# Encoder layer on one core: the projection's begin in another order, softmax reciprocals stored as rows, the output norm in place

## The chip, the cores and the metric

The kernel runs on one NeuronCore of a Trainium2 chip. The metric is the device time of one execution in microseconds (us). In the text PE is TensorE, DVE is VectorE, ACT is ScalarE, POOL is GpSimd, and SP is the engine whose only work here is to issue DMAs; its queue and POOL's are the two queues of data transfers.

## The reference, cut to what matters

One encoder layer over 1024 "sample" and 512 "prompt" tokens of width 1024, in float32, after an input layer norm:

```python
x = LN(x; ln_in)                                      # input norm
u, q_lat, kv_lat, k_rope = split(x @ w_in)            # 512 + 384 + 256 + 32 columns
pool = pool_mixer(u)                                  # windows of 2, 4, 8, 16 tokens
attn = 8-head attention(rms(q_lat) @ w_uq, rms(kv_lat) @ w_ukv, rope)   # softmax
x = LN(alpha*x + [pool | attn] @ w_o; ln1)
aff = softmax(x @ w_router); each of 16 experts takes its top tokens
x = LN(alpha*x + sum over experts of gate * FFN(x); ln2)                # output norm
```

## The kernel before, in words

The program has four phases, one after the other, each with its own order of work written out by hand for each engine; engines meet only at semaphores, and between phases at a barrier. Tokens are worked on in 12 tiles of 128. Every float32 product is made of three passes (`three_passes`, L74 to L76): each operand is rounded to a "hi" part by ACT, and DVE subtracts to get the rest, the "lo" part; hi by hi, hi by lo and lo by hi are summed. So each operand costs an ACT copy and a DVE subtraction ahead of its matmuls.

**Projection** (`phase_project`). SP loads x in tiles, the norm's gain and bias (both spread to 128 partitions), and `w_in` in eight pieces of 128 rows (592 KB each) through a ring of five slots: piece c may only be loaded when DVE is done with piece c-5 (`load_w`). DVE takes a tile's statistics (L370, L373), POOL turns the variance into a reciprocal deviation (L248, L250), DVE normalises in two instructions (L381: subtract the mean and scale by the deviation; L384: multiply by the gain), and POOL adds the bias (L254). PE transposes the tile (L499), ACT rounds the transposed tile (L293), DVE takes its rest (L390). ACT rounds each piece of `w_in` (L299) and DVE takes its rest (L447); the transposed tiles 0 and 1 are rounded after pieces 3 and 6. Then PE makes, for each block of two tiles, the latents of each tile (`latents`, 48 matmuls: two halves of columns, eight pieces each, three passes) and the inputs of the pool mixer (`pool_inputs`, 48 matmuls a half), and transposes the latents (L538), for which DVE scales them (`scale_latents`, L397 to L412) with factors that POOL makes (`latent_rms`, L258, L260). The first product of latents waits for the pieces' rests one by one. The blocks are run in a hardware loop of two passes of two blocks, and a last pair written out.

**Attention** (`phase_attention`) goes over four pairs of heads, three in a hardware loop and one written out, in 20 steps a pair. The probabilities are not normalised: DVE stores the reciprocals of the row sums into `inv_sum`, a token per partition (`rest_probsT`, L940). After each of the six blocks of 512 queries SP stores the block's output (L745) and then its reciprocals, 128 partitions x 4 numbers, to `inv` in device memory (L751). There each number stands by itself: 24 such transfers of 512 numbers of 4 bytes.

**Mix** (`phase_mix`) loads the attention's output and the reciprocals, now as rows spread to 64 partitions (`load_mix`, L1266, L1269), multiplies them on DVE (L1418), and makes the product with `w_o` (loaded at L1277, rounded by ACT at L1378, rest by DVE at L1435). Norm, router and top-k follow.

**Experts** (`phase_experts`) ends with the output norm (`OutputNorm`). Its 12 tiles are read from `acc` in device memory (L1712) into six slots and written by DVE into six others: DVE takes statistics (L1794, L1797) and makes (a - mean) * gain (L1803), POOL the reciprocal deviation (L1729, L1731), then either ACT scales (L1779) and POOL adds the bias (L1738), or, for tiles 3, 8 and 11, DVE does both at once (L1812). For tiles 2, 5, 7 and 10 ACT makes the statistics (`sums`, L1760 to L1764). SP loads tile t+6 when tile t's product is made, and behind each such load stands the store of tile t (L1717) in SP's queue, which waits for that tile to be finished.

Of the kernel before, what the change touches and what calls it, by code (L numbers as in the profile page):

```python
# [87 lines left out]
def phase_project(nc, ident, dram, late, handed):  # L88

    with ExitStack() as ctx:  # L90
# [37 lines left out]
        consts_loaded, ln_loaded = m.sem("a_consts_loaded"), m.sem("a_ln_loaded")  # L128
        w_loaded = [m.sem(f"a_w_loaded{s}") for s in range(RING)]
# [19 lines left out]
        X0T_AFTER = (3, 6)  # L149
# [7 lines left out]
        def _(sp):  # L157
# [3 lines left out]
            for s in range(2):  # L161
                load_x(dram["x_sample"][s * P:(s + 1) * P, :], s)
# [11 lines left out]
            for dst, name in ((ln_g, "ln_in_g"), (ln_b, "ln_in_b")):  # L174
                sp.dma_start(dst[:, :], dram[name].partition_broadcast(P)).then_inc(ln_loaded, 16)
# [7 lines left out]
            for c in range(RING, KD + KVT_):  # L183
                load_w(c)
# [6 lines left out]
            def x_moves(j, s):  # L191

                if j + 1 < N_BLOCKS:
                    sp.wait_ge(x_centred, 2 * j + s + 1)
                    load_x(rows_of(2 * j + 2 + s), s)
# [44 lines left out]
        def _(pool):  # L240
# [11 lines left out]
            def add_bias(j, s):  # L252
                pool.wait_ge(x_scaled, 2 * j + s + 1)
                pool.tensor_tensor(x0[:, s, :], x0[:, s, :], ln_b[:, :], ALU.add).then_inc(x0_done, 1)  # L254
# [10 lines left out]
            pool.wait_ge(ln_loaded, 32)  # L265
            for s in range(2):
                add_bias(0, s)
            for s in range(2):
                reciprocal_std(1, s)
            add_bias(1, 0)  # L270
# [13 lines left out]
            with pool.Fori(0, PAIRS - 1) as i:  # L284
                step(i)
# [3 lines left out]
        def _(act):  # L289
# [6 lines left out]
            for c in range(KD + KVT_):  # L296
# [3 lines left out]
                else:  # L300
                    act.activation(wv_hi[:, c - KD, :], w_raw[:, c % RING, 0:512], ACT.Copy).then_inc(w_hi_done, 1)
                if c in X0T_AFTER:
# [34 lines left out]
            def step(i, last=False):  # L337
                for b in range(2):
# [3 lines left out]
                    for s in range(2):  # L342
# [3 lines left out]
                        round_x0T(j + 1, s, 1 - b)  # L346
                    for s in range(2):
                        copy_v(j, s, ps_u[s])

            with act.Fori(0, PAIRS - 1) as i:  # L350
# [12 lines left out]
        def _(dve):  # L363
# [74 lines left out]
            for s in range(2):  # L438
                statistics(0, s)
            dve.wait_ge(filled, 4)  # L440
            dve.wait_ge(ln_loaded, 32)
            for s in range(2):
                normalise(0, s)
            for c in range(KD + KVT_):
# [7 lines left out]
                if c in X0T_AFTER:  # L452
                    rest_x0T(0, X0T_AFTER.index(c), 0)
            dve.wait_ge(consts_loaded, 64)
            for s in range(2):
                statistics(1, s)
            normalise(1, 0)

            def step(i, positions, last=False):
                for b in range(2):  # L460
                    j = 2 * i + b
                    final = last and b == 1
                    scale_latents(j, 0, positions + 2 * b)
                    if not final:
# [6 lines left out]
                    rest_qT(j, 0)  # L471
                    if not final:
# [13 lines left out]
            with dve.Fori(0, PAIRS - 1) as i:  # L486
# [4 lines left out]
        def _(pe):  # L491
# [11 lines left out]
            def latents(j, s, slot):  # L503
# [5 lines left out]
                for h, (c0, c1) in enumerate(((POOL_DIM, POOL_DIM + SPLIT), (POOL_DIM + SPLIT, IN_DIM))):  # L509
                    for k in range(KD):  # L510
                        if isinstance(t, int) and t == 0 and h == 0:
                            pe.wait_ge(w_lo_done, k + 1)
# [66 lines left out]
            with pe.Fori(0, PAIRS - 1) as i:  # L579
# [13 lines left out]
def phase_attention(nc, ident, dram, late, handed):  # L593

    with ExitStack() as ctx:
# [36 lines left out]
        def half_place(n, h):  # L632
# [16 lines left out]
        row_sum, inv_sum = m.sb("row_sum", [P, 4]), late.inv_sum  # L649
# [36 lines left out]
            m.sem("b_" + x) for x in ("o_done", "inv_done", "o_low_copied", "o_added"))  # L686
        o_stored = [m.sem(f"b_o_stored{s}") for s in range(2)]
# [1577 lines left out]
```

## Time and profile before

| what | value |
| --- | --- |
| times of three runs | 1364.32, 1365.85, 1369.1 us; median 1365.85 us |
| the profiled execution | 1366.01 us, of which the span of its instructions is 1363.9 us |
| mean granted clock of PE | 0.95 |
| PE busy | 1195.7 us, 88% of the span |
| DVE, ACT, POOL busy | 67%, 50%, 27% of the span |
| projection, about | 2 to 232 us |
| attention, about | 233 to 596 us |
| mix, router and top-k, about | 597 to 848 us |
| experts, about | 848 to 1318 us |
| output norm, about | 1318 to 1364 us |

A busy share is a mean over stages with different limits; what a change is worth is read in its own stage, from who waits for whom. Times in the rows are us from the start of the span.

### The profile page before, as it was taken

What the parts mean: (1) busy time and instruction counts of PE and PEld (TensorE: products, weight loads), DVE (VectorE), ACT (ScalarE), POOL (GpSimd) and SP (SyncE); (2) the same over time, 40 slices, a digit from 0 to 9 for tenths busy, and PEclk for the clock granted to TensorE, in tenths of its full rate; (3) what the DMA queues carried; (4) which work ended last, traced back from release to release, by engine and by line L of the source; (5) the groups of instructions that cost most, each with busy time, mean ns of one, the idle gap of its engine ahead of it and who ended that gap; (6) DMA issues with size and microseconds to landing.
All of it is one profiled execution on the core that took longest, in us unless ns stands there. A gap on an engine that the chain in (4) does not pass through costs nothing. (4 is left out here: it accounts for less than half of the span.)

```text
span 1363.9 us, 22070 instructions
## 1 busy us (share of the span) xinstructions
PE 1195.7 (88%) x7370; PEld 1073.6 (79%) x7370; DVE 920.3 (67%) x1539; ACT 684.9 (50%) x1183; POOL 372.7 (27%) x437
## 2 busy tenths in 40 slices
PE   3899997799999999949999962999999999999950
PEld 2899987588788888837787741999999999999940
DVE  7555542477878778746545785777777777777746
ACT  4222221366666676633222222766666666766634
POOL 2222210233523000001221115333334333334217
PEclk9999998799999999979999975999999999999985
DMA  8244463955525111039545453898888998888747
GB/s 260 91 151 150 150 222 134 336 77 102 84 57 84 17 35 32 9 87 285 158 153 163 153 204 96 254 273 283 270 253 275 266 277 281 267 254 274 192 126 268
DMA packets 173743, 242.18 MB, mean 178 GB/s; under 512 B 25856, under 2 KB 135936, under 8 KB 173696
## 3 DMA queue, kind: packets, MB, share of 16 engines
q1 hardware_dynamic: 163840, 206.97, 48.2%
q0 software_dynamic: 9856, 34.61, 11.4%
q8 instruction: 26, 0.43, 0.2%
q14 instruction: 21, 0.17, 0.1%
HBM read 179.37 MB, written 62.18 MB: 177 GB/s over the span
## 5 line engine op out<-in xcount | busy, mean ns | idle before, releaser
L2125 PE MATMUL ps_gate_up<-xT_hi_lo,w_hi 128*128 128x384 f32 x896 | 261.3, 355 | 1.4 <-DVE xT_hi_lo L2050 1.4
L2126 PE MATMUL ps_gate_up<-xT_hi_lo,w_lo 128*128 128x192 f32 x896 | 224.5, 251 | 0.0
L2045 DVE TENSOR_TENSOR w_lo<-w_raw,w_hi 128x2048 fp32r<-128x2048 f32 x93 | 212.2, 2282 | 0.0
L1985 ACT ACTIVATE w_hi<-w_raw 128x2048 fp32r<-128x2048 f32 x92 | 175.7, 1910 | 0.0
L2126 PEld LDWEIGHTS ps_gate_up<-xT_hi_lo,w_lo 128*128 128x128 f32 x896 | 170.7, 191 | 0.6
L2125 PEld LDWEIGHTS ps_gate_up<-xT_hi_lo,w_hi 128*128 128x128 f32 x896 | 168.7, 188 | 2.3 <-issue 1.6
L931 DVE TENSOR_REDUCE neg_max<-ps_scores 128x1 f32<-128x1024 f32 (+1 forms) x80 | 97.6, 1220 | 41.6 <-PE ps_scores L76 41.1
L831 ACT ACTIVATE pT_hi<-ps_probsT 128x512 fp32r<-128x512 f32 x160 | 87.0, 596 | 71.6 <-PE ps_probsT L1058 71.2
L1901 POOL TENSOR_TENSOR d_wait_carrier<-d_zero 128x1 f32<-128x1 f32 x78 | 33.5, 429 | 289.1 <-PE ps_xT L2114 148.0
L944 DVE TENSOR_TENSOR pT_lo<-ps_probsT,pT_hi 128x512 fp32r<-128x512 f32 x160 | 101.3, 673 | 3.9 <-ACT pT_hi L831 3.9
L840 ACT ACTIVATE probs<-ps_scores,neg_max 128x1024 f32<-128x1024 f32 (+1 forms) x96 | 93.5, 979 | 14.6 <-DVE neg_max L931 14.3
L74 PE MATMUL ps_mix<-w_hi,mix_hi 128*128 128x512 f32 x192 | 79.6, 414 | 21.6 <-DVE w_lo L1435 18.6
L1058 PEld LDWEIGHTS ps_probsT<-ident,probs 128*128 128x128 f32 x640 | 72.7, 140 | 26.9 <-DVE pT_lo L944 14.6
L1058 PE MATMUL ps_probsT<-ident,probs 128*128 128x128 f32 x640 | 84.0, 274 | 10.7 <-ACT probs L840 9.9
L75 PE MATMUL ps_mix<-w_lo,mix_hi 128*128 128x512 f32 x192 | 76.2, 397 | 0.0
L76 PE MATMUL ps_mix<-w_hi,mix_lo 128*128 128x512 f32 x192 | 76.1, 396 | 0.0
L74 PE MATMUL ps_scores<-k_hi,q_hi 128*128 128x512 f32 x160 | 65.3, 408 | 1.6 <-DVE q_lo L925 1.6
L74 PE MATMUL ps_lat<-w_in_hi,x0T_hi 128*128 128x384 f32 (+1 forms) x192 | 63.0, 328 | 4.0 <-DVE k_rope_twice L412 3.4
L75 PE MATMUL ps_scores<-k_lo,q_hi 128*128 128x512 f32 x160 | 63.6, 397 | 0.0
L76 PE MATMUL ps_scores<-k_hi,q_lo 128*128 128x512 f32 x160 | 63.2, 395 | 0.0
L75 PE MATMUL ps_lat<-w_in_lo,x0T_hi 128*128 128x384 f32 (+1 forms) x192 | 61.8, 322 | 0.0
L76 PE MATMUL ps_lat<-w_in_hi,x0T_lo 128*128 128x384 f32 (+1 forms) x192 | 61.4, 320 | 0.0
(268 smaller groups left out, 3146.6 us busy)
## 6 DMA issues: line engine op xcount, KB each, us to landing
w_raw<-in_w_gate SPq DMA_DIRECT2D x32, 1024.0 KB, 8.1
w_raw<-in_w_up SPq DMA_DIRECT2D x32, 1024.0 KB, 8.5
w_raw<-in_w_down SPq DMA_DIRECT2D x32, 1024.0 KB, 7.0
scratch_x<-x SPq DMA_DIRECT2D x24, 512.0 KB, 2.7
scratch_v<-v_out SPq DMA_DIRECT2D x12, 512.0 KB, 4.8
v_hi_lo<-scratch_v SPq DMA_DIRECT2D x8, 768.0 KB, 13.0
x_again<-scratch_x SPq DMA_DIRECT2D x12, 512.0 KB, 3.7
scratch_acc<-acc_out SPq DMA_DIRECT2D x12, 512.0 KB, 3.1
```

The source lines that it names most:

```text
L74: nc.tensor.matmul(out, a_hi, b_hi, start=first, stop=False)
L75: nc.tensor.matmul(out, a_hi, b_lo, start=False, stop=False)
L76: return nc.tensor.matmul(out, a_lo, b_hi, start=False, stop=last)
L831: act.activation(pT_hi[unit % 2][half_place(n, h)], ps_t[h][:, :].rearrange("p (k t) -> p k t", t=P), ACT.Copy).then_inc(t_hi_done, 1)
L840: last = act.activation(probs[:, n % 2, x * width:(x + 1) * width], ps_s[n % 2][:, x * width:(x + 1) * width], ACT.Exp, bias=neg_max[:, n ...
L931: nc.vector.tensor_reduce(neg_max[:, n % 2, 0:count], ps_s[n % 2][:, :].rearrange("p (x c) -> p x c", x=count), op=ALU.max, axis=AX.X, neg ...
L944: nc.vector.tensor_tensor(pT_lo[unit % 2][at], ps_t[h][:, :].rearrange("p (k t) -> p k t", t=P), f32(pT_hi[unit % 2][at]), ALU.subtract).t ...
L1058: last = nc.tensor.transpose(ps_t[h][:, k * P:(k + 1) * P], probs[:, n % 2, (4 * h + k) * P:(4 * h + k + 1) * P], ident[:, :])
L1985: act.activation(w_hi[c][:, :], raw[:, c, :], ACT.Copy).then_inc(hi_done, 1)
L2045: nc.vector.tensor_tensor(w_lo[c][:, :], raw[:, c, :], f32(w_hi[c][:, :]), ALU.subtract).then_inc(lo_done, 1)
L2125: nc.tensor.matmul(ps[:, 0:2 * N], w_hi[chunk][:, at], xT[:, k, :], start=k == 0, stop=False)
L2126: nc.tensor.matmul(ps[:, 0:N], w_lo[chunk][:, at], xT[:, k, 0:N], start=False, stop=False)
```

## The change

It has four parts.

1. **The projection's begin.** SP's loads are in another order: tile 0 of x, gain, bias, tile 1, five pieces of `w_in`, then tiles 2 and 3 of x between the other pieces; the tables and gains of the latents and the two pieces for the values come behind. Tiles 0 and 1 are normalised on DVE alone, in two instructions of another kind: (x - mean) * gain, then times the deviation plus bias. The transposed tiles 0 and 1 are rounded after pieces 0 and 3. The first latents take both halves of columns for each piece. The pieces for the values are rounded inside the first block. POOL makes the first latents' factors ahead of the bias of tile 2.
2. **Projection without a hardware loop:** all blocks are written out.
3. **Reciprocals as rows.** `inv_sum` is kept for a whole pair of heads; PE transposes it at the pair's end, ACT copies the 24 x 128 result from PSUM, and SP stores it in one transfer of 24 rows of 512 bytes: 4 transfers instead of 24.
4. **The output norm in place.** Twelve slots, one for each tile, in which all its steps work; SP issues all loads, then all stores. ACT makes the statistics of tiles 2, 4, 6, 8 and 10, DVE ends tiles 3, 6, 9 and 11.

The instructions of DVE at the projection's begin, before (ps_transpose is the transposed tile, w_in_lo the pieces' rests, w_v_lo those of the pieces for the values):

```order
L381 TENSOR_SCALAR x<-x_in,ln_moments,ln_rstd 128x1024
L384 TENSOR_TENSOR x<-x,ln_in_g_all 128x1024
L447 TENSOR_TENSOR w_in_lo<-w_in_raw,w_in_hi 128x1184 x4
L390 TENSOR_TENSOR x0T_lo<-ps_transpose,x0T_hi 128x4x128 x2
L447 TENSOR_TENSOR w_in_lo<-w_in_raw,w_in_hi 128x1184 x3
L390 TENSOR_TENSOR x0T_lo<-ps_transpose,x0T_hi 128x4x128 x2
L447 TENSOR_TENSOR w_in_lo<-w_in_raw,w_in_hi 128x1184
L450 TENSOR_TENSOR w_v_lo<-w_in_raw,w_v_hi 128x512 x2
```

And in the changed program:

```order
L460 SCALAR_TENSOR_TENSOR x<-x_in,ln_moments,ln_in_g_all 128x1024
L466 SCALAR_TENSOR_TENSOR x<-x,ln_rstd,ln_in_b_all 128x1024
L381 BN_STATS ln_stats<-x_in 128x6 x2
L81 MEMSET wait_carrier 128x1
L384 BN_AGGR ln_moments<-ln_stats 128x2
L460 SCALAR_TENSOR_TENSOR x<-x_in,ln_moments,ln_in_g_all 128x1024
L452 TENSOR_TENSOR w_in_lo<-w_in_raw,w_in_hi 128x1184
L466 SCALAR_TENSOR_TENSOR x<-x,ln_rstd,ln_in_b_all 128x1024
L401 TENSOR_TENSOR x0T_lo<-ps_transpose,x0T_hi 128x4x128 x2
L452 TENSOR_TENSOR w_in_lo<-w_in_raw,w_in_hi 128x1184 x3
L401 TENSOR_TENSOR x0T_lo<-ps_transpose,x0T_hi 128x4x128 x2
L452 TENSOR_TENSOR w_in_lo<-w_in_raw,w_in_hi 128x1184 x4
```

The rests of tile 0 moved from behind four pieces to behind one, those of tile 1 from behind seven to behind four, and the pieces for the values moved out of this stretch.

SP's issues at the end of the attention, last pair, and the mix's first loads, before:

```order
L745 DMA scratch_mixT<-uT_then_o_out 64x512
L751 DMA scratch_inv<-inv_sum 128x4x1
L595 UNCONDITIONAL_BRANCH
L1258 UNCONDITIONAL_BRANCH
L1266 DMA mix_raw<-scratch_mixT 128x4x128
L1269 DMA inv_rows<-scratch_inv 64x4x128 x2
L1277 DMA w_raw<-in_w_o 128x1024 x2
```

And in the changed program:

```order
L793 DMA scratch_mixT<-uT_then_o_out 64x512 x5
L791 DMA scratch_inv<-inv_row 24x128
L793 DMA scratch_mixT<-uT_then_o_out 64x512
L637 UNCONDITIONAL_BRANCH
L1310 UNCONDITIONAL_BRANCH
L1318 DMA mix_raw<-scratch_mixT 128x4x128
L1323 DMA inv_rows<-scratch_inv 64x4x128 x2
L1331 DMA w_raw<-in_w_o 128x1024 x2
```

The store of reciprocals moved ahead of the last store of outputs, and is one transfer of rows.

The diff, cut to its core:

```diff
@@ phase_project, sync
-            for s in range(2):
-                load_x(dram["x_sample"][s * P:(s + 1) * P, :], s)
...
+            load_x(dram["x_sample"][0:P, :], 0)
+            for dst, name, loaded in ((ln_g, "ln_in_g", ln_g_loaded), (ln_b, "ln_in_b", ln_loaded)):
+                sp.dma_start(dst[:, :], dram[name].partition_broadcast(P)).then_inc(loaded, 16)
+            load_x(dram["x_sample"][P:2 * P, :], 1)
             for c in range(RING):
                 load_w(c)
+            for s in range(2):
+                sp.wait_ge(x_centred, s + 1)
+                load_x(dram["x_sample"][(2 + s) * P:(3 + s) * P, :], s)
+                load_w(RING + s)
+            load_w(RING + 2)
...
@@ phase_project, gpsimd
                 for b in range(2):
                     j = 2 * i + b
                     latent_rms(j, 0)
+                    if j == 0:
+                        add_bias(1, 0)
+                        reciprocal_std(1, 1)
...
-            with pool.Fori(0, PAIRS - 1) as i:
+            for i in range(PAIRS - 1):
                 step(i)
@@ phase_project, vector
+            def centre_first(s):
+                dve.wait_ge(stats_done, s + 1)
+                nc.vector.scalar_tensor_tensor(out=x0[:, s, :], in0=x_in[:, s, :], scalar=moments[:, s, 0:1], in1=ln_g[:, :],
+                                               op0=ALU.subtract, op1=ALU.mult).then_inc(x_centred, 1)
+            def finish_first(s):
+                dve.wait_ge(rstd_done, s + 1)
+                dve.wait_ge(x_centred, s + 1)
+                nc.vector.scalar_tensor_tensor(out=x0[:, s, :], in0=x0[:, s, :], scalar=rstd[:, s:s + 1], in1=ln_b[:, :],
+                                               op0=ALU.mult, op1=ALU.add).then_inc(x0_done, 1)
...
+            statistics(1, 0)
+            normalise(1, 0)
@@ phase_project, tensor: latents
+                if t == 0:
                     for k in range(KD):
+                        pe.wait_ge(w_lo_done, k + 1)
+                        for h, (c0, c1) in enumerate(halves):
+                            last = three_passes(...)
...
@@ phase_attention, sync
+                    if b == BLOCKS - 1:
+                        sp.wait_ge(inv_copied, i + 1)
+                        heads = bass.ds(2 * i if last else sp.snap(2 * i), 2)
+                        sp.dma_start(dram["inv"][heads, :].rearrange("h (t p) -> (h t) p", p=P), inv_row[:, :]).then_inc(inv_stored, 16)
...
-                    with nc.allow_non_contiguous_dma("a float per row, once a block"):
-                        sp.dma_start(of_head.rearrange("h (t p) -> p (h t)", p=P)[:, tiles], inv_sum[:, head, tiles]).then_inc(inv_stored[head][blk], 16)
@@ phase_attention, scalar
+            def copy_inverses(i):
+                act.wait_ge(inv_turned, i + 1)
+                act.wait_ge(inv_stored, 16 * i)
+                act.activation(inv_row[:, :], ps_q[inv_as_rows], ACT.Copy).then_inc(inv_copied, 1)
...
@@ phase_attention, tensor: end of a pair
                 outputs(i, UNITS - 2)
+                pe.wait_ge(inv_done, STEPS * i + STEPS)
+                pe.wait_ge(q_rotated, BLOCKS * i + (BLOCKS if last else BLOCKS + 1))
+                pe.wait_ge(o_added, UNITS * i + UNITS - 2)
+                nc.tensor.transpose(ps_q[inv_as_rows], inv_sum[:, :, :].rearrange("p h t -> p (h t)"), ident[:, :]).then_inc(inv_turned, 1)
                 if not last:
                     key_block(i + 1, 2)
                 outputs(i, UNITS - 1)
-                pe.wait_ge(o_added, UNITS * i + UNITS - 2)
@@ phase_mix, sync: load_mix
+                if isinstance(s, int) and s == 0:
+                    sp.wait_ge(late.inv_stored, 16 * N_HEADS // 2)
@@ OutputNorm
-    SUMS_ON_SCALAR = (2, 5, 7, 10)
-    ENDS_ON_VECTOR = (3, 8, 11)
+    SUMS_ON_SCALAR = (2, 4, 6, 8, 10)
+    ENDS_ON_VECTOR = (3, 6, 9, 11)
...
     def load(self, sp, t):
-        if t >= self.SLOTS:
-            sp.wait_ge(self.z_done, t - self.SLOTS + 1)
...
         def product(t):
-            if t >= self.SLOTS:
-                dve.wait_ge(self.stored[t % self.SLOTS], 16 * (t // self.SLOTS))
...
@@ phase_experts, sync
-            for t in range(norm.SLOTS, N_TILES):
+            for t in range(N_TILES):
                 if t == SAMPLE_TILES:
                     sp.wait_ge(scattered[1], 16 * N_EXPERTS)
                 norm.load(sp, t)
-                norm.store(sp, t - norm.SLOTS)
-            for t in range(N_TILES - norm.SLOTS, N_TILES):
+            for t in range(N_TILES):
                 norm.store(sp, t)
```

## Rows read from the trace of the kernel before

**Rows 1.** Windows over the projection: length, busy time (instructions), clock, DMA share, GB/s

```profile
26.00:45.20 19.20, 15.07 (x101) 14.55 (x100) 13.67 (x25) 5.70 (x11) 6.17 (x7) 1.00 0.67 213
45.20:62.00 16.80, 16.77 (x114) 16.78 (x115) 7.50 (x15) 3.21 (x10) 3.28 (x3) 0.90 0.18 64
62.00:94.00 32.00, 32.00 (x233) 31.46 (x232) 17.36 (x40) 8.19 (x23) 8.01 (x10) 1.00 0.47 161
```

**Rows 2.** Timeline, projection's begin: start, us, engine, line, operation, tiles [idle before]

```profile
5.15 1.28 DVE L370 BATCH_NORM_STATS2 ln_stats<-x_in 128x6 f32<-128x512 f32 x2 [5.15 <-DMA x_in<-in_x_sample]
...
10.93 0.81 DVE L381 TENSOR_SCALAR x<-x_in,ln_moments,ln_rstd 128x1024 f32<-128x1024 f32 x1 [2.85 <-issue]
...
12.56 1.19 ACT L299 ACTIVATE w_in_hi<-w_in_raw 128x1184 fp32r<-128x1184 f32 x1 [9.47 <-DMA w_in_raw<-in_w_in]
...
14.05 1.19 ACT L299 ACTIVATE w_in_hi<-w_in_raw 128x1184 fp32r<-128x1184 f32 x1 [0.29 <-DMA w_in_raw<-in_w_in]
...
16.94 7.44 DVE L447 TENSOR_TENSOR w_in_lo<-w_in_raw,w_in_hi 128x1184 fp32r<-128x1184 f32 x4
...
24.30 1.27 DVE L390 TENSOR_TENSOR x0T_lo<-ps_transpose,x0T_hi 128x512 fp32r<-128x512 f32 x2
24.41 3.05 SPq L172 DMA_DIRECT2D w_in_raw<-in_w_ukv  x2
...
25.50 3.98 DVE L447 TENSOR_TENSOR w_in_lo<-w_in_raw,w_in_hi 128x1184 fp32r<-128x1184 f32 x3
...
28.75 0.43 SPq L197 DMA_DIRECT2D scratch_x<-x  x1
```

**Rows 3.** DMA issues of 0 to 35 us: count, KB, median us to landing

```profile
scratch_x<-x SPq DMA_DIRECT2D x2, 512.0 KB, 7.1
```

**Rows 4.** Timeline, where PE goes on after its first gap

```profile
43.57 0.62 DVE L397 TENSOR_SCALAR lat_scaled<-ps_lat,lat_rms 128x384 f32<-128x384 f32 x1 [3.72 <-POOL lat_rms L260]
...
45.23 0.77 PE L538 MATMUL ps_latT_q_rope<-ident,lat_scaled 128*128 128x128 f32 x3 [3.51 <-DVE k_rope_twice L412]
```

**Rows 5.** Timeline, from the attention's last stores to the mix's first matmul

```profile
595.34 0.47 SPq L745 DMA_DIRECT2D scratch_mixT<-uT_then_o_out  x1
595.85 0.59 SPq L751 DMA_DIRECT2D scratch_inv<-inv_sum  x1
597.02 0.38 SPq L1266 DMA_DIRECT2D mix_raw<-scratch_mixT  x1
...
609.30 0.69 DVE L1418 TENSOR_TENSOR mix_raw<-mix_raw,inv_rows 128x512 f32<-128x512 f32 x1 [13.99 <-DMA inv_rows<-scratch_inv]
...
613.01 0.77 PE L74 MATMUL ps_mix<-w_hi,mix_hi 128*128 128x512 f32 x1 [18.57 <-DVE w_lo L1435]
```

**Rows 6.** Window behind the last store of reciprocals

```profile
599.00:606.00 7.00, 0.00 (x0) 0.00 (x0) 0.00 (x0) 0.00 (x0) 0.60 (x2) 0.50 0.27 39
```

**Rows 7.** DMA queue of 597.0 to 597.3 us: packets, MB, share of 16 engines

```profile
q1 hardware_dynamic: 305, 0.01, 64.4%
```

**Rows 8.** DMA issues of 640 to 760 us

```profile
inv_rows<-scratch_inv SPq DMA_DIRECT2D x16, 128.0 KB, 4.0
```

**Rows 9.** Groups of the output norm: busy us, mean ns, idle before and releaser

```profile
L1803 DVE SCALAR_TENSOR_TENSOR w_raw<-w_raw,ln_moments,ps_xT 128x1024 f32<-128x1024 f32 x12 | 14.7, 1249 | 0.0
L1794 DVE BATCH_NORM_STATS2 ln_stats<-w_raw 128x6 f32<-128x512 f32 x16 | 10.2, 680 | 10.9 <-DMA w_raw<-scratch_acc 10.9
L1764 ACT ACTIVATE ps_y_sample<-w_raw,ln_minus_mean 128x1024 f32<-128x1024 f32 x4 | 4.5, 1118 | 0.1
L1738 POOL TENSOR_TENSOR w_raw<-w_raw,ln_b_all 128x1024 f32<-128x1024 f32 x9 | 21.0, 2349 | 1.3 <-ACT w_raw L1779 1.3
```

**Rows 10.** Timeline, the output norm's first statistics and last steps

```profile
1323.35 1.28 DVE L1794 BATCH_NORM_STATS2 ln_stats<-w_raw 128x6 f32<-128x512 f32 x2 [6.89 <-DMA w_raw<-scratch_acc]
...
1354.40 4.93 SPq L1717 DMA_DIRECT2D y_prompt<-w_raw  x4
1355.67 1.28 DVE L1812 SCALAR_TENSOR_TENSOR w_raw<-w_raw,ln_rstd,ps_gate_up 128x1024 f32<-128x1024 f32 x1
```

More of the change, by code:

```diff
@@ L264, in _ @@
                 reciprocal_std(0, s)
[L265 to L270, printed above, removed]
+            pool.wait_ge(ln_loaded, 16)
+            reciprocal_std(1, 0)
             def step(i, last=False):
@@ L301, in _ @@
                     act.activation(wv_hi[:, c - KD, :], w_raw[:, c % RING, 0:512], ACT.Copy).then_inc(w_hi_done, 1)
+            for c in range(KD):
+                round_w(c)
                 if c in X0T_AFTER:
@@ L346, in step @@
                         round_x0T(j + 1, s, 1 - b)
+                        if j == 0 and s == 0:
+                            for c in range(KD, KD + KVT_):
+                                round_w(c)
                     for s in range(2):
                         copy_v(j, s, ps_u[s])
-            with act.Fori(0, PAIRS - 1) as i:
+            for i in range(PAIRS - 1):
                 step(i)
@@ L436, in rest_v, with rest_w @@
                                         f32(v_out[:, s, :, 0, :]), ALU.subtract).then_inc(v_lo_done, 1)
[L438 to L444, printed above, removed]
+            def rest_w(c):
                 dve.wait_ge(w_hi_done, c + 1)
@@ L471, in step @@
                     rest_qT(j, 0)
+                    if j == 0:
+                        for c in range(KD, KD + KVT_):
+                            rest_w(c)
                     if not final:
@@ L484, in step @@
                         normalise(j + 2, 0)
-            with dve.Fori(0, PAIRS - 1) as i:
+            for i in range(PAIRS - 1):
                 step(i, 4 * i)
@@ L577, in step @@
                     pe.wait_ge(v_lo_done, 2 * j + 1)
-            with pe.Fori(0, PAIRS - 1) as i:
+            for i in range(PAIRS - 1):
                 step(i)
@@ L1119, in __init__ @@
         self.o_late_stored = [m.sem(f"o_late_stored{x}") for x in range(2)]
[L1120 removed]
+        self.inv_stored = m.sem("inv_stored")
         self.done_with = []
@@ L1298, in step @@
                         sp.wait_ge(late.o_late_stored[1], 16 * N_HEADS // 2)
-                        for h in range(2):
-                            sp.wait_ge(late.inv_stored[h][2], 16 * N_HEADS // 2)
                     load_d(s + 2, slot)
@@ L1304, in step @@
                         sp.wait_ge(late.o_late_stored[0], 16 * N_HEADS // 2)
-                        for h in range(2):
-                            sp.wait_ge(late.inv_stored[h][1], 16 * N_HEADS // 2)
                 if not isinstance(s, int) or 0 < s < N_TILES - 1:
@@ L1675, in __init__ @@
         rows = experts.raw[:, :, :].rearrange("p c (h d) -> p (c h) d", d=D)
-        self.a, self.y = [rows[:, b, :] for b in range(self.SLOTS)], [rows[:, self.SLOTS + b, :] for b in range(self.SLOTS)]
+        self.rows = [rows[:, t, :] for t in range(N_TILES)]
         self.ln_g, self.ln_b = m.sb("ln2_g_all", [P, D]), m.sb("ln2_b_all", [P, D])
@@ L1755, in sums @@
     def sums(self, act, t):
-        a, done = self.a[t % self.SLOTS], 3 * self.SUMS_ON_SCALAR.index(t)
+        a, done = self.rows[t], 3 * self.SUMS_ON_SCALAR.index(t)
         self.wait_loaded(act, t)
@@ L1884, in _ @@
             sp.wait_ge(scattered[0], 16 * N_EXPERTS)
-            for t in range(norm.SLOTS):
-                norm.load(sp, t)
-            for t in range(norm.SLOTS, N_TILES):
+            for t in range(N_TILES):
                 if t == SAMPLE_TILES:
@@ L1890, in _ @@
                 norm.load(sp, t)
-                norm.store(sp, t - norm.SLOTS)
-            for t in range(N_TILES - norm.SLOTS, N_TILES):
+            for t in range(N_TILES):
                 norm.store(sp, t)
-            for b in range(norm.SLOTS):
-                sp.wait_ge(norm.stored[b], 16 * N_TILES // norm.SLOTS)
+            sp.wait_ge(norm.stored, 16 * N_TILES)
         @block.gpsimd
```

102 lines of the change are left out of this document (58 added, 44 removed).

## The prediction

> **What bounds the kernel now.** I read the windows first, to see which engine fills a stage, and then, at the three places that the change touches, the timeline with its releasers. In the projection PE is the bound once it is under way: from 62 us it is busy 32.00 us of 32.00, at 0.137 us a matmul (32.00 / 233), at its upper level of 2.4 GHz [rows 1]. So this stage can only gain at its begin. From 26.00 to 45.20 PE is busy 15.07 of 19.20 us, and the gap of 3.51 us up to 45.23 ends with DVE's scaled latents, which waited for POOL [rows 1, 4]. From 45.20 to 62.00 the granted clock is 0.90: a tenth of 16.80 us, 1.7 us, goes to a stretch at 1.2 GHz behind that gap [rows 1]. At the change from attention to mix PE waits 18.57 us, to 613.01; ahead of it DVE waits 13.99 us, to 609.30, for the reciprocals' rows [rows 5]. While it waits, from 599 to 606, the DMA engines are busy 0.27 and move 39 GB/s [rows 6]: the transfers are slow, not many. In the output norm DVE is the longest engine, and it stands still 10.9 us for loads: 6.9 before the first tile, the other 4.0 in the middle [rows 9, 10].
>
> **Part 1, the projection's begin.** I follow DVE, since all its pieces are known. Tile 0 is there at 5.15, gain and bias before were at 10.93 [rows 2]. A piece of 592 KB comes every 1.49 us (12.56 to 14.05), so 512 KB take 1.29 [rows 2]; with tile 1 moved behind the bias, the bias is there at 9.6, tile 1 at 10.9 and piece 0 at 12.5 as before. For the gain I take 7.7. Statistics of a tile take two times 0.68 and a short rest, 1.5; the new instructions have the kind and size of L1803, 1.25 each [rows 9]. Tile 0: statistics to 6.7, first step 7.7 to 8.95, second 9.65 to 10.9. Tile 1: statistics to 12.4, first step to 13.65. Rest of piece 0 (ACT has rounded it at 13.75): 3.98 / 3 = 1.33 [rows 2], to 15.1; second step to 16.3; rest of transposed tile 0: 1.27 [rows 2], to 17.6; three pieces to 21.6; tile 1 to 22.9; four pieces to 28.2. Before, four of these rests cost 7.44 us beside POOL's bias instead of 5.3 [rows 2]; no bias of POOL's runs there now. PE makes the six matmuls of the last piece by 29.0 (0.82), and the 48 of the pool inputs by 35.6 (6.6).
>
> What is late next is the normalised tile 2, in which DVE overwrites tile 0's place, so that tile 0 must have been stored. Before, the store was issued at 28.75, behind the two loads for the values (24.41 and 3.05 on) and a load of x [rows 2]; now that load is gone, and the two loads wait for the rest of piece 4 at 24.2, so I put the store at 25.8. Two stores took 7.1 in the median [rows 3]: 32.9. Normalising takes 0.81 [rows 2] and about 1.2 (as L1803), to 34.95; the scaled latents 1.66 (43.57 to 45.23 [rows 4]), to 36.6. POOL's factors don't hold them, since they now stand ahead of a bias of 2.35 [rows 9]; that bias, done at 37.3, meets PE as it ends the six transposes of the latents at 37.4. So PE goes on at 36.6 instead of 45.23, 8.6 earlier, after a gap of 1.0 and not 3.5, behind which I expect no stretch at 1.2 GHz: 1.7 more. I take 10.0 of these 10.3. Bounds: if the store lands as late as before (28.75 + 7.1 = 35.85), PE goes on at 39.6 and the clock falls: 5.7; if nothing but PE's own work counts, 35.6: 11.3.
>
> The trace speaks for the level staying up: PE has pieces with gaps before 45.20 too, and its clock there is 1.00 [rows 1]. The Trainium skill ("TensorE: Matmul & The Clock Gate", section "A second HAM failure mode: psum-queue depth-cycling") says that many short idle times between groups of matmuls can make the clock swing between its levels, and PE now gets six matmuls for every 1.33 us. By that rule six take 1.65 us at the low level, the latents end at 32.6 and PE goes on at 39.2, so this part would be 2.6 us smaller.
>
> **Part 2, no loop.** PE is full through the loop's turn, so there is nothing to take: 0. What it could cost is code loading, of which PE's full windows show none.
>
> **Part 3, reciprocals as rows.** At the phase's change SP's last issue is now the store of outputs; with the barrier as before the first load goes out at 596.4 instead of 597.02 [rows 5]. ACT's copy and the store stand ahead of the last outputs, so the wait for the store's landing (less than the 4.0 us of [rows 8], an estimate from that row) ends about there. The two loads of rows are issued by 597.5, and where no scatter stands ahead such a load lands 4.0 us after its issue [rows 8], at 601.5; before it was 609.30. PE's first matmul hangs on `w_o`, which stands next in the queue, and comes as much earlier: 7.7. PE's four added transposes are about one matmul of [rows 1] each, 0.14, on PE's path in three pairs; ACT's copies stand in its waits for outputs. 7.7 - 0.4 = 7.3, and I take 7.0. The other 23 stores of single numbers had nothing of PE's behind them: 0. The four new waits of PE ask for reciprocals, rotated queries and added outputs of steps that PE's outputs already follow. Bounds: 0.2 (only the 0.6 of SP's end, less 0.4) and 7.7.
>
> That the slow seven microseconds are the scatter's is read from its place alone. The Trainium skill ("DMA: Bandwidth & Descriptors", section "Why small descriptors are slow (HBM only)") gives small descriptors a fixed cost each on their way, a few cycles and 32 bytes. By that rule the 512 numbers cost what their packets last: 0.644 x 16 x 0.3 us / 305 = 10 ns each [rows 7], 0.3 us over 16 engines, and this part would be worth 0.5. The rows speak against it, since the engines idle after the packets have ended [rows 6].
>
> **Part 4, output norm.** Loads no longer wait for products, so the 4.0 us of idle time fall away and DVE is bound by its own work: 7 statistics of 1.45, 12 products in 14.7, 4 ends of 1.28 [rows 9, 10] = 10.2 + 14.7 + 5.1 = 30.0, from 1323.35 to 1353.3 instead of 1356.95. ACT has 5 sums of two passes of 1.12 and short rests (2.7) and 8 scalings, each like one such pass, 22.6; POOL 8 biases of 2.35, 18.8, and small ones: both fit under 30. The last store was issued by 1359.33 [rows 10], behind POOL's last bias; now by 1353.8: 5.5. Bounds: 3.0 (DVE waits 2.5 us for ACT's sums), 6.0.
>
> **Sum.** 10.0 + 7.0 + 5.5 = 22.5. The profiled execution took 1366.01 (span 1363.9 and 2.1 around it), 0.16 over the median of the runs: 1366.0 - 22.5 = 1343.5 us. All lower bounds: 5.7 + 0.2 + 3.0 = 8.9, 1357.1. All upper: 25.0, 1341.0.
>
> **The rivals.** (a) The slow stretch at 597 isn't the scatter's: it starts at the barrier too, where all loads begin at once; the transfers themselves are few, which speaks against. Part 3 is 0.2: 1350.3. (b) The store of tile 0 lands as late as before, because the weights' last pieces and the narrow loads stand ahead of it: the same queue and kinds are there, but one load less. Part 1 is 5.7: 1347.8. (c) DVE isn't the bound of the output norm, as 12 stores behind 12 loads end later or ACT's sums come late: 3.0 there, 1346.0. (d) Slower: PE, fed piece by piece from the start, stays at 1.2 GHz far into the projection. A matmul then costs 0.137 us more; the gain is gone after 22.5 / 0.137 = 164 matmuls at the low level, and with 200 it is slower by 0.3%; with 400, 1376. Against it: the low stretch behind the gap at 41.7 cost 1.7 us, 12 matmuls' worth.
>
> **How the numbers follow.** Forecast 0.62 (1340 to 1348, as parts 1 to 4 miss a little either way); (a) 0.14; (b) 0.11; (c) 0.06; (d) 0.03; several lower bounds together 0.04. The range: the upper bounds' 1341.0, less 1.5 for the runs' spread below their median, 1339.5; above, (a) and a small miss in another part, 1352.5; outside stay (d), sums of lower bounds and a part of (a), under 0.2. Faster by over 0.3% (4.1 us, about what a measurement of this kernel tells from no change) means under 1361.8: all but (d) and a rest, 0.95; within 0.3%: 0.02; slower: 0.03.
>
> **What would show it.** In the changed profile: the rest of the last `w_in` piece ends by 28.2; PE's gap before the first transposes of latents is near 1 us and ends near 36.6; no slow stretch of DMA behind the barrier, and DVE's first product of the mix about 5 us after it; in the output norm no DVE wait for a load but the first, and 30 us from its first statistics to its last end. Wrong: PE waiting for weights in the first latents, the rows' landing holding SP at the barrier, or the clock at 1.2 GHz in the projection.

## The result, and the profile after

The changed kernel takes 1349.28 us in the median of four runs (1348.19 to 1353.78), the kernel before 1367.05; the ratio is 0.987 (0.985 to 0.989). A second set of six runs gave 1348.84 against 1367.5, ratio 0.988 (0.9855 to 0.990). So it is 17.8 to 18.7 us faster, where 22.5 were forecast; 1343.5 was predicted, 1339.5 to 1352.5 the range. The profile of the changed kernel is that of its slowest execution, 1353.78 us; a second one, of an execution of 1347.73 us, follows under a_repeat.

**The projection's begin** went nearly as worked out. The windows of the changed kernel (columns as in [rows 1]):

```profile
26.00:36.00 10.00, 8.60 (x64) 7.92 (x62) 7.96 (x15) 2.38 (x6) 4.46 (x5) 1.00 0.60 199
36.00:45.00 9.00, 8.92 (x62) 8.93 (x63) 7.51 (x14) 3.93 (x10) 3.14 (x3) 1.00 0.46 173
45.00:62.00 17.00, 17.00 (x121) 16.48 (x120) 11.95 (x28) 4.68 (x12) 2.81 (x7) 1.00 0.03 10
```

And its timeline there, answering to [rows 2, 4]:

```profile
26.25 1.30 SPq L203 DMA_DIRECT2D scratch_x<-x  x2
...
27.50 1.39 DVE L452 TENSOR_TENSOR w_in_lo<-w_in_raw,w_in_hi 128x1184 fp32r<-128x1184 f32 x1 [0.94 <-ACT w_in_hi L304]
...
36.08 0.55 PE L580 MATMUL ps_latT_q_rope<-ident,lat_scaled 128*128 128x128 f32 x3 [0.24 <-DVE k_rope_twice L423]
```

The last rest ends at 28.9 (28.2 was expected), the stores of x go out at 26.25 (25.8), and PE goes on at 36.08 (36.6) instead of 45.23, after a gap of 0.24 us instead of 3.51. From there it is full, and the stretch at 1.2 GHz behind the old gap is gone: 1.00 where [rows 1] had 0.90. One wait was another than expected: the store of tile 0 had landed at 30.26 (32.9 was expected), and DVE's normalising of tile 2 began at 31.33 behind POOL's deviation. So DVE came to the scaled latents at 33.32 and not 34.95, but took 2.8 us for them (to 36.08) and not 1.66: two misses that nearly cancel.

**The end of the attention** lost its slow stretch. Timeline of the changed kernel, and the window that answers to [rows 6]:

```profile
592.65 0.47 SPq L793 DMA_DIRECT2D scratch_mixT<-uT_then_o_out  x1
593.77 0.42 SPq L1318 DMA_DIRECT2D mix_raw<-scratch_mixT  x1
...
600.59 0.69 DVE L1468 TENSOR_TENSOR mix_raw<-mix_raw,inv_rows 128x512 f32<-128x512 f32 x1 [7.96 <-DMA inv_rows<-scratch_inv]
...
604.29 0.76 PE L74 MATMUL ps_mix<-w_hi,mix_hi 128*128 128x512 f32 x1 [12.53 <-DVE w_lo L1485]
```

```profile
596.00:603.00 7.00, 0.00 (x0) 0.00 (x0) 1.46 (x3) 1.57 (x2) 0.34 (x2) 0.50 0.93 261
```

PE's wait is 12.53 us and not 18.57 [rows 5]; behind the last store the DMA engines move 261 GB/s, where it was 39 [rows 6].

**The output norm** is DVE's own work now. Groups of the changed kernel's output norm (columns as in [rows 9]) and its last steps:

```profile
L1787 POOL TENSOR_TENSOR w_raw<-w_raw,ln_b_all 128x1024 f32<-128x1024 f32 x8 | 18.8, 2353 | 0.2 <-ACT w_raw L1824 0.2
L1848 DVE SCALAR_TENSOR_TENSOR w_raw<-w_raw,ln_moments,ps_xT 128x1024 f32<-128x1024 f32 x12 | 14.7, 1252 | 0.0
L1824 ACT ACTIVATE w_raw<-w_raw,ln_rstd 128x1024 f32<-128x1024 f32 x8 | 9.0, 1138 | 2.7 <-DVE w_raw L1848 2.7
L1841 DVE BATCH_NORM_STATS2 ln_stats<-w_raw 128x6 f32<-128x512 f32 x14 | 8.9, 679 | 7.3 <-DMA w_raw<-scratch_acc 7.3
```

```profile
1317.45 1.29 DVE L1841 BATCH_NORM_STATS2 ln_stats<-w_raw 128x6 f32<-128x512 f32 x2 [7.27 <-DMA w_raw<-scratch_acc]
...
1344.05 2.47 DVE L1857 SCALAR_TENSOR_TENSOR w_raw<-w_raw,ln_rstd,ps_gate_up 128x1024 f32<-128x1024 f32 x2
```

DVE waits once, for the first tile, and is done 29.1 us after it began (30.0 expected; before 33.6).

These three are worth what the forecast said. What it had not seen stands in the middle. Attention starts 11.0 us earlier than before (first product of PE at 227.26, before 238.25), but PE's last product of it starts at 591.48, only 2.7 earlier: it takes 364.2 us instead of 355.9. Compared instruction by instruction, 3.3 us of this are lost up to DVE's `wq_lo` near 317 us, and 4.7 within the next 11 us; 1.8 of the 3.3 already stand at 271 us, before DVE's first long subtraction. The changed kernel there, first DVE, then POOL, then PE (a single row), then the windows:

```profile
314.34 2.38 DVE L973 TENSOR_TENSOR q_lo<-q_work,q_hi 128x512 fp32r<-128x512 f32 x1
316.65 2.74 DVE L954 TENSOR_TENSOR wq_lo<-wq_wide,wq_hi 128x384 fp32r<-128x384 f32 x1
319.31 1.21 DVE L979 TENSOR_REDUCE neg_max<-ps_scores 128x1 f32<-128x1024 f32 x1
```

```profile
314.27 1.91 POOL L833 TENSOR_TENSOR window_a<-window_b 128x1033 f32<-128x1033 f32 x1
316.26 2.71 POOL L833 TENSOR_TENSOR window_b<-window_a 128x1025 f32<-128x1025 f32 x1
319.05 2.54 POOL L838 TENSOR_TENSOR window_b<-window_b,inv_count 128x1024 f32<-128x1024 f32 x1
```

```profile
321.89 1.97 PE L1107 MATMUL ps_probsT<-ident,probs 128*128 128x128 f32 x8 [3.45 <-ACT probs L882]
```

```profile
317.00:320.00 3.00, 1.43 (x6) 0.83 (x5) 3.00 (x2) 0.00 (x0) 2.92 (x2) 1.00 0.03 5
320.00:323.00 3.00, 1.11 (x5) 1.12 (x6) 3.00 (x6) 1.21 (x2) 2.92 (x2) 0.58 0.19 44
323.00:326.00 3.00, 3.00 (x10) 2.52 (x10) 1.69 (x4) 2.53 (x6) 1.74 (x3) 0.50 0.19 75
```

And the kernel before at the same place of the program:

```profile
322.79 1.67 DVE L925 TENSOR_TENSOR q_lo<-q_work,q_hi 128x512 fp32r<-128x512 f32 x1
324.38 0.55 DVE L906 TENSOR_TENSOR wq_lo<-wq_wide,wq_hi 128x384 fp32r<-128x384 f32 x1
```

`q_lo` and `wq_lo` are DVE subtractions whose two inputs both lie in SBUF. Alone they take 0.68 and 0.55 us; beside POOL's window sums, which read and write SBUF, 2.38 and 2.74, and each then ends about half a us behind a POOL instruction's end. `neg_max`, which reads PSUM, takes 1.21 beside POOL as without it. The softmax's maximum waits behind the two, PE waits 3.45 us, and from 320.5 us on, within that gap, its clock is at 1.2 GHz for 6.8 us. In the kernel before `q_lo` met POOL too (1.67), `wq_lo` did not. The Trainium skill ("SBUF — State Buffer", section "SBUF: two separate sides") states that DVE and GpSimd share one pair of ports as an exclusive lock, which a DVE instruction with two SBUF inputs needs. The trace agrees: 0.55 alone, 2.74 beside POOL.

Why did POOL's sums stand there now? Because their inputs land sooner. POOL's first step of the group of sums near 310 us, before and in the changed kernel:

```profile
313.07 1.91 POOL L783 TENSOR_TENSOR window_a<-u_in 128x1039 f32<-128x1039 f32 x1 [13.10 <-DMA inv_count<-in_inv_count]
```

```profile
310.28 1.91 POOL L825 TENSOR_TENSOR window_a<-u_in 128x1039 f32<-128x1039 f32 x1 [4.13 <-DMA inv_count<-in_inv_count]
```

And the DMA issues of 236 to 450 us (count, KB, median us to landing), b_proj (below), which keeps the stores of single numbers, and the changed kernel:

```profile
u_in<-scratch_uT POOLq DMA_DIRECT2D x4, 512.0 KB, 10.3
```

```profile
u_in<-scratch_uT POOLq DMA_DIRECT2D x4, 512.0 KB, 4.7
```

### The profile page after: what moved, and what is told of

Read it like the earlier page. It is cut to its first block and busy times, and to the rows that moved or that the text cites. A ratio compares the mean times of both kernels' runs of the same rounds, so it can differ in the third digit from the quotient of the medians.

```text
span 1352.0 us, 21821 instructions
## 1 busy us (share of the span) xinstructions
PE 1200.3 (89%) x7374; PEld 1076.7 (80%) x7374; DVE 920.6 (68%) x1536; ACT 686.6 (51%) x1191; POOL 363.4 (27%) x434
## 5 line engine op out<-in xcount | busy, mean ns | idle before, releaser
L882 ACT ACTIVATE probs<-ps_scores,neg_max 128x1024 f32<-128x1024 f32 (+1 forms) x96 | 93.5, 978 | 16.1 <-DVE neg_max L979 15.9
L1107 PEld LDWEIGHTS ps_probsT<-ident,probs 128*128 128x128 f32 x640 | 73.5, 141 | 28.6 <-DVE pT_lo L991 16.9
L2108 DVE TENSOR_TENSOR gate<-ps_gate_up,gate_rest 128x192 f32<-128x192 f32 x64 | 22.9, 357 | 57.1 <-ACT gate_rest L2043 54.9
```

The costliest lines, as they stand in the source:

```text
L882: last = act.activation(probs[:, n % 2, x * width:(x + 1) * width], ps_s[n % 2][:, x * width:(x + 1) * width], ACT.Exp, bias=neg_max[:, n ...
L1107: last = nc.tensor.transpose(ps_t[h][:, k * P:(k + 1) * P], probs[:, n % 2, (4 * h + k) * P:(4 * h + k + 1) * P], ident[:, :])
```

## The experiments

Theory A: part 3 takes 24 slow stores away from the DMA engines; POOL's loads land in half the time, its sums move against DVE's steps and meet the SBUF subtractions; attention pays. B: the loss comes of the earlier start. C: it is part 3's own waits and transposes on PE. The kernels (medians; "att. starts": PE's first product of the attention; "lasts": to the start of its last one; "gap": from there to the mix's first product; "norm": from the output norm's first statistics to the end; "excess": what DVE's subtractions and copies within SBUF took in the attention over their time alone, where it was over 0.3 us; "pair": from the attention's 17th `neg_max` to its 20th, the stretch with the two subtractions shown above; "low": clock at 1.2 GHz from 30 us behind the attention's start to its end; all but the medians from one profile each, us):

| kernel | median | att. starts | lasts | gap | norm | excess | pair | low |
| --- | --- | --- | --- | --- | --- | --- | --- | --- |
| before | 1366.8 to 1367.6 | 238.3 | 355.9 | 18.8 | 40.5 | 5.6 | 12.6 | 0 |
| k_before_again | 1367.78 | 233.2 | 359.9 | 18.5 | 41.0 | 6.0 | 12.4 | 0 |
| after | 1349.28 | 227.3 | 364.2 | 12.8 | 34.5 | 8.1 | 18.0 | 6.8 |
| a_repeat (after) | 1348.84 | 227.5 | 359.3 | 12.3 | 34.5 | 7.5 | 16.1 | 3.4 |
| b_proj | 1356.20 | 226.7 | 357.9 | 19.6 | 41.0 | 8.2 | 13.4 | 0 |
| c_rows | 1364.99 | 236.1 | 363.4 | 12.6 | 40.6 | 6.0 | 18.1 | 6.8 |
| d_norm | 1360.10 | 236.9 | 354.9 | 18.8 | 34.5 | 3.8 | 12.2 | 0 |
| e_one_scatter | 1351.99 | 225.9 | 359.5 | 19.1 | 34.5 | 7.6 | 15.3 | 0 |
| f_all_scatters | 1351.25 | 224.2 | 359.6 | 20.4 | 34.5 | 4.3 | 11.8 | 3.4 |
| g_paced | 1343.20 | 224.7 | 357.0 | 12.5 | 34.5 | 1.4 | 11.8 | 0 |
| h_unrolled | 1362.53 | 236.3 | 354.4 | 18.7 | 41.0 | 2.9 | 12.1 | 0 |
| l_unrolled_again | 1365.94 | 235.2 | 355.4 | 20.0 | 40.9 | 4.8 | 11.9 | 0 |
| i_warm | 1343.63 | 228.4 | 355.1 | 12.6 | 34.5 | 1.4 | 11.7 | 0 |
| j_warm_both | 1342.49 | 225.4 | 356.4 | dummies | 34.5 | 1.4 | 11.8 | 0 |

**a_repeat**: the changed kernel, not edited. 

> The changed kernel once more, for a second profile of it and a tighter ratio. In its first profile (1353.8 us) attention started 11.0 us earlier than before but PE's last product of it came only 2.9 us earlier, and another 2.9 went at the experts' start, where PE stayed longer at 1.2 GHz. Theory A (POOL's windows run sooner without the scatters and meet DVE's subtractions of tiles in SBUF; how badly differs from execution to execution): about 1349 us; attention takes 357 to 365 us instead of 356.2, POOL's loads of u_in again land within 5 us, and if a q_lo or wq_lo of over 2 us shows again, a PE gap of some us stands behind it. Theory B (the loss belongs to the earlier start and is the same in each execution): attention again 364 us. Theory C (the loss is the four added waits of PE at the pairs' ends): the loss is in four equal steps at the pairs' ends.

The same collision is there (`wq_lo` 2.75 us), but attention took 359.3 us: how much it costs differs by execution, so B's constant 364 falls. The loss falls in no four equal steps at the pairs' ends: from the 41st `neg_max` on, with two of the four ends in it, the attention takes 162.0 us in both profiles of the changed kernel, and 161.7 to 163.1 in the six of kernels without part 3. C falls.

**b_proj, c_rows, d_norm**: the kernel before with the diff's projection (parts 1, 2), its attention and mix (part 3) and its `OutputNorm` (part 4) alone.

> The kernel before with parts 1 and 2 alone (the projection in the new order, written out). All theories: PE goes on after its first gap at about 36.1 us, attention starts 10.9 us earlier. Theory A: attention as long as before (356 us), since the scatters stay, the total 10 to 12 us less (1355 to 1357). Theory B: attention takes up to 8 us longer, the total only 3 to 6 us less.

> The kernel before with part 3 alone (reciprocals as rows). Theory A: PE's first matmul of the mix comes 5.8 us sooner after the attention's last product than before; POOL's loads of u_in and inv_count land in 4 to 6 us instead of 8 to 16, its windows shift against DVE, and attention is longer by 0 to 8 us: total between 6 us less and 2 us more. Theory B: attention as long as before, total 5 to 7 us less. Theory C: each pair longer by the same 1 to 2 us.

> The kernel before with part 4 alone (the output norm in place). All theories: nothing ahead of the output norm changes; DVE has no wait for a load but the first, 29 to 30 us from its first statistics to its last end; the total is 5.5 to 6.5 us less (1360).

The ratios are 0.993 (0.991 to 0.995), 0.998 (0.996 to 1.000) and 0.995 (0.994 to 0.997): 11.3, 2.5 and 7.4 us less. b_proj starts attention as early as the changed kernel and keeps its length: B is out. c_rows has the new, shorter gap and the long attention at once, with the collision at the same instructions. c_rows, DVE:

```profile
323.68 2.25 DVE L931 TENSOR_TENSOR q_lo<-q_work,q_hi 128x512 fp32r<-128x512 f32 x1
325.85 2.73 DVE L912 TENSOR_TENSOR wq_lo<-wq_wide,wq_hi 128x384 fp32r<-128x384 f32 x1
```

So the loss came with part 3: it gains 6.3 us at the phase's change and gives most of it back 270 us earlier.

**e_one_scatter**: one store of single numbers back, for nobody.

```diff
+            with nc.allow_non_contiguous_dma("a float per row, read by nobody"):
+                sp.dma_start(dram["unread"][7:8, :].rearrange("h (t p) -> p (h t)", p=P)[:, 8:12], ident[:, 8:12]).then_inc(late.unread_stored, 16)
             for s in range(2):
                 sp.wait_ge(o_stored[s], 32 * PAIRS)
```

> The changed kernel with one more store: 512 single numbers (constants) behind the last store of outputs, to a place that nobody reads and for which nobody waits at the phase's change. Theory 1 (a store of single numbers holds up what is issued behind it on all DMA engines): the first loads of the mix land some 6 us later, PE's gap ahead of its first matmul of the mix is 18 to 20 us and not 12.5, total 6 us more than the changed kernel, about 1355. Theory 2 (only who reads the very numbers has to wait for them, or the slow loads came of the barrier): the gap stays 12.5 to 13.5, the total within 1 us of the changed kernel's.

Windows and PE's row in its profile:

```profile
590.00:597.00 7.00, 0.00 (x0) 0.00 (x0) 0.00 (x0) 0.00 (x0) 0.81 (x3) 0.50 0.22 33
```

```profile
604.55 0.77 PE L74 MATMUL ps_mix<-w_hi,mix_hi 128*128 128x512 f32 x1 [18.82 <-DVE w_lo L1489]
```

The slow stretch is back (33 GB/s; [rows 6] had 39), with the gap of 19 us, though nobody reads those 2 KB, and SP asks for their landing only behind the loads of tile 3, near 624 us, when they have long landed (596). Theory 1 holds for the gap; the total rose 3.2 us, not 6: beside a_repeat's profile attention starts 1.6 us earlier and the stages behind the mix's first product take 1.7 less, which is as much as two profiles of one kernel differ by.

**f_all_scatters**: such a store, of constants, at all 24 old places.

```diff
                         o_late_stored[b - 4] if b >= 4 else o_stored[b % 2], 16)
+                    sp.wait_ge(inv_done, STEPS * i + last_step[2 * b + 1] + 1)
+                    of_head = bass.ds(2 * i + head if last else sp.snap(2 * i + head), 1)
+                    ...
+                        sp.dma_start(dram["unread"][of_head, :].rearrange("h (t p) -> p (h t)", p=P)[:, tiles], ident[:, tiles]).then_inc(late.unread_stored, 16)
```

> The changed kernel with 24 stores of 512 single numbers back at the places in SP's queue where the kernel before had them, of constants and to a place that nobody reads; the reciprocals still go as rows. Theory A (without such stores POOL's loads land sooner, its windows run beside DVE's subtractions in SBUF, and these take up to 2.7 us): POOL's loads land in 8 to 12 us again, q_lo and wq_lo near 315 us take under 2 us, attention takes 355 to 358 us instead of 359 to 364; with the gap at its end back at 19 us the total is 1350 to 1354. Rival (attention is longer by part 3's transposes, waits and copies): attention stays at 359 to 364 us, the total is 1355 or more.

POOL's loads of `u_in` land in 11.8 us again, and `q_lo` and `wq_lo` near 311 us take 0.68 and 0.55. So the single-number stores by themselves set when POOL's loads land, and the stretch "pair" takes 11.8 us, as in g_paced below. But the attention lasted 359.6: another pair met POOL (1.79 and 1.65 us, near 396). Its length is therefore a miss of Theory A; where a collision falls is not told by the stores alone. The total lies in the range given.

**g_paced**: the collision itself taken away, by where POOL's sums begin.

```diff
+            WINDOWS_AFTER = (2, 5, 7, 8, 11, 13, 14, 17)
...
+                    pool.wait_ge(q_lo_done, WINDOWS_AFTER[loads - 1])
                     pool.wait_ge(u_loaded, 16 * loads)
```

> The changed kernel with one wait more for each of POOL's eight window sums: they begin behind a given q_lo of DVE (the 2nd, 5th, 7th, 8th, 11th, 13th, 14th, 17th), in stretches where DVE subtracts no tile in SBUF. Theory A: no q_lo, wq_lo, wk_lo or wq_wide of DVE beside a window sum, each at 0.7 us or less, no PE gap of over 1 us in attention, attention 354 to 357 us, total 3 to 6 us less than the changed kernel, 1343 to 1346. Rival (the loss is part 3's own instructions, or the clock's state by itself): attention stays at 359 or more, total as the changed kernel's.

Its DVE at the same place, and one POOL row with the new wait:

```profile
311.36 0.68 DVE L975 TENSOR_TENSOR q_lo<-q_work,q_hi 128x512 fp32r<-128x512 f32 x1
311.95 0.55 DVE L956 TENSOR_TENSOR wq_lo<-wq_wide,wq_hi 128x384 fp32r<-128x384 f32 x1
```

```profile
327.52 1.91 POOL L827 TENSOR_TENSOR window_a<-u_in 128x1039 f32<-128x1039 f32 x1 [16.14 <-DVE q_lo L975]
```

1343.2 us, ratio to before 0.982 (0.980 to 0.985), below both kernels: 5.6 less than the changed kernel, with all of part 3's instructions in place. One subtraction is still met (`q_lo` of 2.12 us at 356.6), the rest are undisturbed, attention lasts 357.0 and the clock stays up in it. i_warm and j_warm_both below have the same waits and came out as low. Pacing was not tried on the kernel before, whose subtractions meet POOL as well (excess 5.6): part of the gain may be there too.

**h_unrolled, l_unrolled_again, k_before_again**: part 2 alone (`with x.Fori(0, PAIRS - 1) as i:` of four engines made `for i in range(PAIRS - 1):`), twice, and the kernel before against itself.

> The kernel before with part 2 alone: the projection's loops of POOL, ACT, DVE and PE written out, nothing else. As predicted (PE is full through the loop's turn): within 1.5 us of the kernel before. Rival (the loop's turns cost PE, or code loading costs the longer program): over 2 us either way, seen in PE's gaps between 62 and 200 us.

> The kernel before itself, for a second profile and as a measure of what a comparison of two equal kernels gives: h_unrolled came out 4.3 us faster than the kernel before, with nothing in its profile at the loop's turn that tells why. If comparisons drift by that much, this one differs by 2 to 4 us too; if not, it is within 1.5 us, and those 4.3 us are real and open. In its profile the projection's begin shows whether the 2 us by which h_unrolled, c_rows and d_norm all started attention earlier than the first profile of before were that execution's own.

> h_unrolled once more (part 2 alone, the kernel before with the projection's loops written out), for a second profile and a second ratio. A comparison of the kernel before with itself gave 1.000, so its 4.3 us (0.9954 to 0.9986) are more than such a comparison drifts by itself. If part 2 has a worth of its own: again 3 to 5 us less than before. If it was those executions' draw (how often the clock dips and how POOL's windows meet DVE): within 2 us. In the profile, the projection of h_unrolled and of before take the same time where both have the clock's two short dips.

The first gave 0.997 (0.9954 to 0.9986), the repeat of the same kernel 0.9996 (0.998 to 1.001), before against itself 1.0004 (0.9986 to 1.002). So the 4.3 us can't be put down to part 2, and one comparison's interval is narrower than what separates two of them, here 3.5 us; by themselves the totals of c_rows and e_one_scatter weigh little. Attention, which follows the loops, starts at 235.7 us in the mean of the two profiles without them and at 236.1 in the four of the kernel before, k_before_again, c_rows and d_norm: no worth of part 2 can be told, as predicted.

**i_warm, j_warm_both**: dummy transposes behind g_paced's lists, and also at the mix's begin.

```diff
             last.then_inc(lists_turned, 1)
+            for x in range(44):
+                nc.tensor.transpose(ps_mix[0][:, 0:P], ident[:, :], ident[:, :])
```

> g_paced with 44 transposes of no use, of the identity into a bank of PSUM that is no longer read, on PE behind its last transposes of the top-k lists, in its wait of some 9 us ahead of the experts. In every profile with part 3 PE's clock came back to 2.4 GHz 3.3 to 6.1 us after the first product of the experts, in every one without it 1.3 to 1.9 us ahead of it, with the same instructions and the same waits of PE in front. Theory 1 (those 2 us, from the first product to DVE's first gate in 4.5 to 5.0 us and not 2.9, are the clock's alone): with PE busy through the wait the clock is at 2.4 GHz at the first product, the first gate comes 2.9 us or less after it, total 2 to 4 us less than g_paced, 1339 to 1341. Theory 2 (the experts' first weights or rows come later with part 3): the clock is up and the gate still comes 4.5 us or more after; total as g_paced, 1343.

> i_warm with 90 more transposes of no use at the mix's begin, in PE's wait of 10 us for the first operands, behind which the clock was at 1.2 GHz for 5 to 6 us. If PE's products there are bound by the clock: 2 to 3 us less than i_warm. Rival (they are bound by the rests of w_o that DVE makes from pieces as they land): within 1 us of i_warm, with longer gaps of PE behind the first products.

1343.63 and 1342.49 us: no gain over g_paced that can be told. In i_warm the clock came up (0.70 over the dummies, 1.00 behind them), PE idled 1.86 and 0.74 us, and at 827.7 it fell again, ahead of the first product; windows of i_warm:

```profile
816.00:824.00 8.00, 7.35 (x46) 7.11 (x46) 1.59 (x9) 0.00 (x0) 2.01 (x2) 0.70 0.32 95
824.00:827.60 3.60, 1.15 (x9) 0.94 (x10) 0.70 (x2) 0.93 (x2) 0.60 (x6) 1.00 0.18 22
827.60:835.00 7.40, 6.04 (x25) 5.67 (x26) 1.44 (x3) 0.98 (x2) 2.78 (x8) 0.54 1.08 357
```

So it doesn't decide between its two theories. That the late clock belongs to part 3 alone fell otherwise: the first gate of the experts came 4.9 and 5.0 us after the first product in k_before_again and l_unrolled_again too, which have no part 3. In the other four without it, it came after 2.9, in all eight with it after 4.5 to 5.0; whether part 3 makes the late clock likelier is open. In j_warm_both PE then waited 1.93 and 1.41 us for DVE's `w_lo` and `mix_lo`: the mix's begin is bound by operands, as its rival said.

## Why the prediction was right in kind and 5 us off in size

- **Part 1, 10.0.** Attention starts at 236.0 us in the mean of the six profiles with the old begin, at 226.2 in the mean of the eight with the new one: 9.8. The order of the steps was as worked out, though the store that was to hold up tile 2 did not. The stretch at 1.2 GHz behind the old gap, worth 1.7, is in four of the six profiles and missing in k_before_again and l_unrolled_again; another, near 200 us, comes and goes with either begin. Where both kinds have the same stretches the new begin is 8.3 and 8.5 us earlier, and 10.0 where the old one has the first in addition; 8.6 and 1.7 had been forecast. The clock did not swing with the many short waits: it is 1.00 from 26 to 36 us, with a wait of 1.14 us ahead of the last piece's products. By the Trainium skill's account of "psum-queue depth-cycling" ("TensorE: Matmul & The Clock Gate", section "A second HAM failure mode: psum-queue depth-cycling") it could have swung. Rivals (b) and (d) are out; (d)'s 1376 us for 400 matmuls at the low level is a slip, by its own 0.137 us it is 1398.
- **Part 2, 0.** Held, as far as can be told.
- **Part 3, the phase's change, 7.0.** The gap is 19.1 us with single numbers (six profiles) and 12.6 with rows (five): 6.5. That the scatter causes the slow stretch had been read from its place alone; e_one_scatter shows it, and rival (a) is out. By the Trainium skill's fixed cost for each small descriptor ("DMA: Bandwidth & Descriptors", section "Why small descriptors are slow (HBM only)"), as the prediction read it, this part was to be worth 0.5; the measurement decides.
- **Part 4, 5.5.** From the first statistics to the end 40.8 us in the mean before, 34.5 now: 6.3, a little over the upper bound of 6.0; DVE's own work took 29.1 and not 30.0. Rival (c) is out.
- **The step that failed** is in part 3: "The other 23 stores of single numbers had nothing of PE's behind them: 0." PE's own operands indeed did not wait for them, but POOL's loads did, and these set when POOL works. With rows the attention lasts 361.6 us in the mean (after, a_repeat, c_rows, e_one_scatter), with single numbers 356.4 (six profiles), with rows and POOL paced 356.1 (g_paced, i_warm, j_warm_both); f_all_scatters, 359.6, has rows and single numbers and is in none of these means. So this term is -5.2 and not 0. Of it 4.4 lie in the stretch "pair": 16.9 us in the mean with rows, 12.5 with single numbers, 11.8 paced. Another 1.1 stand before the attention's 7th `neg_max`, where no subtraction has been long yet and the clock's stretches differ between profiles of one kernel too (1.6 us between the two of the kernel before, 1.9 between the two of the changed one); the rest of the attention gives 0.4 back. Two of the four profiles with rows, those of after and c_rows, are of executions 4.5 and 2.5 us over their kernel's median, so 5.2 is rather too much.

The terms then make 9.8 + 6.5 + 6.3 - 5.2 = 17.4 us; 17.8 and 18.7 were measured. That the time lay in the range all the same is in part luck: no rival and no bound stood for this loss, and it fit into the room left for rival (a). b_proj and f_all_scatters warn against a simple rule: the excess alone does not tell the loss (with 8.2 us of it b_proj's attention is 1.5 longer than the mean of its kind; the changed kernel's 8.1 hold 2.2 of copies, and its 5.8 of subtractions are hardly more than the 5.6 of the kernel before). It costs most where two subtractions are met in a row and PE's gap brings the clock down, as in the changed kernel and c_rows. The wait and the clock can be told apart there: e_one_scatter met the same pair with the clock up, and "pair" took 15.3 us, 3.5 over g_paced; with 3.4 us at 1.2 GHz (a_repeat) it took 16.1, with 6.8 (after, c_rows) 18.0 and 18.1. So the wait is some 3.5 us. Behind the two subtractions, from the 18th `neg_max` to the 20th, e_one_scatter takes 8.1 us, a_repeat 9.6, c_rows 10.8: there the clock costs 1.4 to 2.7.

## What to carry to other kernels

A transfer that nobody seems to wait for still sets when other queues' transfers land; ask whose start moves when it goes, and what those instructions will then run beside. DVE subtractions with both inputs in SBUF and long POOL instructions belong at different times: a wait that holds POOL back, off the critical path, was worth 5.6 us. Store rows of 512 bytes rather than single numbers where anything is loaded soon after.

## What had not been expected of the hardware

- 512 numbers of 4 bytes, whose packets last some 0.3 us over the 16 engines by [rows 7], hold back the loads issued next behind them: the first load of the mix landed 11.7 us after its issue in e_one_scatter, 3.0 in the changed kernel. What holds them is not shown.
- A DVE subtraction of 0.55 us became 2.75 us beside POOL, and POOL's own sum 2.71 instead of 1.91 us.
- The same kernel's attention differs by 5 us between executions, with the collisions and the clock's stretches; the start of the attention differed by 5 us too (233.2 and 238.3 in two profiles of the kernel before). Of the latter 3.4 us are two stretches of 3.4 us at 1.2 GHz, at 45 and 206 us, which the one profile has and the other has not.
